# A layer that starts with four output tiles on unnormalised input, three narrow tiles, and waits that are moved

## What is computed

```python
def hybrid_layer(x, ...):
    proj = x @ w_in                       # 2048 -> 4928 columns
    (q_lat, kv_lat, k_rope, g_mla, p_in, g_pool, c_h, c_b, c_c, g_conv) = jnp.split(proj, ...)
    y_mla = mla_mixer(...) * silu(g_mla)  # latents are rms-normed, projected, 8 heads attend
    y_pool = pool_mixer(...) * silu(g_pool)
    y_conv = conv_mixer(...) * silu(g_conv)
    out = concat([y_mla, y_pool, y_conv]) @ w_out + b_out
    return layernorm(DEEPNORM_ALPHA * x + out, ln_g, ln_b)
```

## Time and profile before

| | us |
|---|---|
| median of three runs | 2517.47 |
| lowest, highest | 2517.44, 2517.75 |
| the profiled execution | 2517.92 |
| its span, first to last instruction | 2516.2 |
| PE busy in the span | 2426.2 (96%) |
| DVE, ACT, POOL busy | 1260.9, 890.5, 396.4 |
| mean granted clock of PE | 0.985 of full |

### The profile page before, as it was taken

The page is one execution under the profiler, slowest core; times in us unless marked ns, Lnnn a source line. Parts: engine busy times, 40 slices in busy tenths (PEclk is TensorE's granted clock), DMA queues, the critical chain, the costliest instruction groups (busy, mean ns, idle before and its releaser), DMA issues.

```text
span 2516.2 us, 31644 instructions
## 1 busy us (share of the span) xinstructions
PE 2426.2 (96%) x11582; PEld 1979.5 (79%) x11582; DVE 1260.9 (50%) x1789; ACT 890.5 (35%) x1344; POOL 396.4 (16%) x391
## 2 busy tenths in 40 slices
PE   4999999999999999999999998899999999999997
PEld 2778888788888778888788886688877888887886
DVE  8655544366446555544366546634245444444334
ACT  4422222365224422223365223422224444444221
POOL 6400000033003300000042003003001122122000
PEclk8999999999999999999999999999999999999999
DMA  3455554212222455553212222323221222222332
GB/s 140 154 168 176 174 178 132 83 59 67 92 92 67 156 175 170 181 181 127 80 55 69 92 90 101 126 92 100 92 92 59 84 75 81 76 76 97 129 100 75
DMA packets 78281, 277.70 MB, mean 110 GB/s; under 512 B 8832, under 2 KB 9088, under 8 KB 77824
## 3 DMA queue, kind: packets, MB, share of 16 engines
q1 hardware_dynamic: 61344, 213.29, 26.5%
q0 software_dynamic: 16864, 63.45, 7.5%
HBM read 268.31 MB, written 8.39 MB: 110 GB/s over the span
## 4 chain that ended last, share of the span: by engine, by line
PE 80%; issue 9%; DVE 6%; POOL 3%; ACT 2%; DMA 0%; DVEq 0%; ACTq 0%; SPq 0%; POOLq 0%
PE bank L309 25%; PE bank L311 25%; PE bank L310 25%; POOL sum L394 1%; DVE w_lo L304 1%; PE bank L1871 1%; DVE x_lo L1024 1%; POOL probs L381 1%; PE bank L1801 1%; ACT w_hi L294 1%; PE bank L1935 0%; DVE x_res L1577 0%; DVE squares L1030 0%; PE bank L1936 0%; PE bank L1786 0%
## 5 line engine op out<-in xcount | busy, mean ns | idle before, releaser
L311 PE MATMUL bank<-x_hi,w_hi 128*128 128x512 f32 x2928 | 1145.0, 391 | 0.0
L310 PE MATMUL bank<-x_hi,w_lo 128*128 128x512 f32 x2928 | 1143.4, 390 | 0.0
L309 PE MATMUL bank<-x_lo,w_hi 128*128 128x512 f32 (+1 forms) x2416 | 966.4, 400 | 33.2 <-DVE x_lo L1024 17.4
L304 DVE TENSOR_TENSOR w_lo<-w_raw,w_hi 128x1024 fp32r<-128x1024 f32 x390 | 491.7, 1263 | 827.0 <-ACT w_hi L294 825.9
L294 ACT ACTIVATE w_hi<-w_raw 128x1024 fp32r<-128x1024 f32 x390 | 407.5, 1048 | 964.9 <-PE bank L311 949.1
L311 PEld LDWEIGHTS bank<-x_hi,w_hi 128*128 128x128 f32 x2928 | 548.4, 187 | 120.6
L310 PEld LDWEIGHTS bank<-x_hi,w_lo 128*128 128x128 f32 x2928 | 549.7, 188 | 113.1 <-issue 2.4
L309 PEld LDWEIGHTS bank<-x_lo,w_hi 128*128 128x128 f32 (+1 forms) x2416 | 453.9, 188 | 132.4 <-issue 33.8
L309 PE MATMUL bank<-mix_lo,w_hi 128*128 128x512 f32 x640 | 252.8, 395 | 1.3 <-issue 1.0
L381 POOL TENSOR_SCALAR probs<-probs,stats 128x128 f32<-128x128 f32 (+3 forms) x128 | 138.7, 1090 | 679.1 <-DVE stats L1312 679.0
L309 PEld LDWEIGHTS bank<-mix_lo,w_hi 128*128 128x128 f32 x640 | 120.7, 189 | 27.2 <-issue 1.6
(11 more groups left out here) (296 smaller groups left out, 2207.5 us busy)
## 6 DMA issues: line engine op xcount, KB each, us to landing
w_raw<-stream SPq DMA_DIRECT2D x390, 512.0 KB, 3.5
ada_w<-wada POOLq DMA_DIRECT2D x96, 512.0 KB, 4.6
x_res<-xT SPq DMA_DIRECT2D x16, 256.0 KB, 5.4
x_res_spill<-x_res POOLq DMA_DIRECT2D x8, 512.0 KB, 7.5
x_res<-x_res_spill POOLq DMA_DIRECT2D x8, 512.0 KB, 7.2
outT<-x_res SPq DMA_DIRECT2D x16, 256.0 KB, 2.3
cond_b<-cond POOLq DMA_DIRECT2D x2, 1024.0 KB, 5.4
row_params<-rows POOLq DMA_DIRECT2D x1, 1536.0 KB, 7.4
```

Of the source, the lines that this page charges most:

```text
L304: nc.vector.tensor_tensor(out=WL[:, slot, :cols[n]], in0=RAW[:, slot, :cols[n]], in1=WH[:, slot, :cols[n]].bitcast(F32), op=ALU.subtract). ...
L309: nc.tensor.matmul(out, wh, xl, start=first, stop=False)
L310: nc.tensor.matmul(out, wl, xh, start=False, stop=False)
L311: return nc.tensor.matmul(out, wh, xh, start=False, stop=last)
```

## The change

**Four raw tiles.** Layer 1 no longer waits for the norm. With g and b the gain and offset of the norm, m the mean and r the inverse deviation of a token, W^T (g (y - m) r + b) = r (W^T (g y) - m W^T g) + W^T b. So tiles 0 to 3 run on g y, split in two parts by ACT (`raw_hi`, during the output tiles) and DVE (`raw_lo`), and DVE (`raw_tile`) and ACT apply m, r and the two weight sums to the results. W^T g and W^T b are made on PE from the unrounded weights, eight units of eight matmuls with two moving columns (`weight_sums`): four in the last two output tiles of layer 0, four in the raw tiles, where the totals and the spreads stand too. Tile 4 is the first on normalised input. Layer 1 swaps the two activation buffers (in its rows `x_lo` holds the rounded part and `x_hi` the rest), and four units of weights instead of three stand at its start.

**The norm's own work.** `x_res` is centred by POOL (14 tiles, `ysub`) ahead of the residual's add, in both layers, so that `centred` and the last correction of the shift leave DVE. In layer 1 a feature tile may be written only when the four raw tiles have used it (`raw_freed`).

**Narrow tiles.** The weights of a narrow tile are packed twice; DVE turns the second copy into the low part in place. One matmul with 128 (or 64) columns then makes hi and lo together, two matmuls per k instead of three, and DVE adds the two row groups afterwards. This concerns `T_KR` in both layers and `T2_F`.

**Waits moved.** The latent sums stand at k = 5 instead of 7 and their spread at 10 instead of 12 (in layer 1 one tile later), those of the second group at 15 instead of 7 and, in the next tile, 6 instead of 2. The spatial products stand at k = 7 to 14 of their tile instead of 0, 2, ..., 14. `q_lo` of the first pair comes before the gates. Slots are counted through, so that a unit waits for the third one before it everywhere.

```diff
+OUT_ORDER = (MIX_ORDER, list(range(16)))
...
+RAW_LAYER, RAW_TILES = 1, 4
+RAW_BANKS = (0, 3, 4, 6)
...
+        HI, LO = (XH, XL, XH), (XL, XH, XL)
+        OFF_HI, OFF_LO = (OFF_XH, OFF_XL), (OFF_XL, OFF_XH)
...
+        def raw_freed(k):
+
+            n = RAW_LAYER * LAYER_UNITS
+            if k % 8 == 7:
+                return w_used, n + RAW_TILES * (k // 8 + 1)
+            return S["raw_used"], k + 1 - k // 8
...
+                wide = narrow(l, s)
+                if wide:
+                    raw, both = (t[:, slot, :].rearrange("p (k c) -> p k c", c=P)[:, :, wide:2 * wide]
+                                 for t in (RAW, WH))
+                    nc.vector.tensor_tensor(out=both, in0=raw, in1=both.bitcast(F32), op=ALU.subtract)\
+                        .then_inc(w_lo, 1)
+                    continue
...
+                pool.wait_ge(S["sh_b"], l + 2)
+                for k in range(2, KT):
+                    nc.gpsimd.tensor_tensor(out=Y[:, k, :], in0=Y[:, k, :], in1=SB[:, :], op=ALU.subtract)\
+                        .then_inc(S["ysub"], 1)
...
+            def raw_hi(n, k):
+                nc.scalar.activation(HI[n][:, k, :], Y[:, k, :], ACT.Copy, scale=norm_cols(n, k)[0])\
+                    .then_inc(S["raw_hi"], 1)
...
+                    act.wait_ge(S["bc_m"], n)
+                    nc.scalar.activation(SB[:, :], PS[2][:, :], ACT.Copy).then_inc(S["sh_tot"], 1)
...
+                    if n == RAW_LAYER and k in (5, 6, 7, 8):
+                        split(n, 2 + (k - 5) // 2, ((k - 5) % 2,))
+                    elif n < DEPTH and n != RAW_LAYER and k in (11, 12):
                         split(n, 2, (k - 11,))
                     buf = NBUF[k % 4]
                     gain, offset = norm_cols(n, k)
                     act.wait_ge(S["n_mul"], KT * n + k + 1)
+                    if n == RAW_LAYER:
+                        act.wait_ge(*raw_freed(k))
...
+                raw = RAW_TILES if l == RAW_LAYER else 0
+                for i in range(raw):
+                    if i == 2:
+                        split(l, 5)
+                        act.wait_ge(S["cond_in"], 16 * (l + 1))
+                        nc.scalar.activation(CONDB[:, :], CONDB[:, :], ACT.Silu).then_inc(S["cond_silu"], 1)
+                        lat_sd(l, 0)
+                        act.wait_ge(S["lat_bc"], 2 * l + 1)
+                    act.wait_ge(S["lat_raw"], 2 * (i + 1))
+                    if i:
+                        act.wait_ge(S["sq_sum"], 4 * l + (0, 0, 1, 1)[i])
+                    nc.scalar.activation((T0, Y1)[i % 2][:, :], LAT[:, i, :], ACT.Square, scale=-1.0,
+                                         bias=VEC[:, 2 * i + 1:2 * i + 2]).then_inc(S["in_ev"], 1)
+                    nc.scalar.activation(LAT[:, i, :], LAT[:, i, :], ACT.Identity, scale=-1.0,
+                                         bias=VEC[:, 2 * i + 1:2 * i + 2]).then_inc(S["lat_hi"], 1)
+                    if i < 2:
+                        split(l, 4, (i,))
...
-                dve.wait_ge(S["bc_m"], n)
-                TT(out=SB[:, :], in0=SB[:, :], in1=PS[2][:, :], op=ALU.add).then_inc(S["sh_tot"], 1)
                 dve.wait_ge(S["bc_r"], n)
+
+            def raw_lo(n, k):
+                dve.wait_ge(S["raw_hi"], k + 1)
+                dve.wait_ge(w_used, n * LAYER_UNITS - (k < 8))
+                STT(out=LO[n][:, k, :], in0=Y[:, k, :], scalar=col(n - 1, C_LG + k), in1=HI[n][:, k, :].bitcast(F32),
+                    op0=ALU.mult, op1=ALU.subtract).then_inc(S["raw_lo"], 1)
+
+            def raw_sums():
+                dve.wait_ge(S["vec_mm"], 2 * RAW_TILES)
+                V.tensor_copy(VEC[:, :], PS[5][:, 2 * RAW_TILES:4 * RAW_TILES]).then_inc(S["vec_set"], 1)
+                dve.wait_ge(S["vec_set"], 1)
+                TT(out=VEC[:, :], in0=PS[5][:, 0:2 * RAW_TILES], in1=VEC[:, :], op=ALU.add).then_inc(S["vec_set"], 1)
+                dve.wait_ge(S["vec_set"], 2)
+
+            def raw_tile(l, t):
+                dve.wait_ge(w_used, first_done(l, t))
+                dve.wait_ge(S["n_x"], norm_uses(l, KT - 1))
+                STT(out=LAT[:, t, :], in0=SB[:, :], scalar=VEC[:, 2 * t:2 * t + 1], in1=PS[RAW_BANKS[t]][:, :],
+                    op0=ALU.mult, op1=ALU.subtract).then_inc(S["lat_raw"], 1)
+                dve.wait_ge(S["lat_raw"], 2 * t + 1)
+                TT(out=LAT[:, t, :], in0=LAT[:, t, :], in1=PS[7][:, :], op=ALU.mult).then_inc(S["lat_raw"], 1)
...
+                if raw:
+                    raw_sums()
+                    raw_tile(l, 0)
+                    split(l, 4, (0,))
+                    raw_tile(l, 1)
+                    split(l, 4, (1,))
+                    raw_tile(l, 2)
+                    raw_tile(l, 3)
+                    split(l, 5)
...
+                V.tensor_copy(LAT[0:ROPE, 6, :], PS[7][ROPE:P, :]).then_inc(S["kr_sum"], 1)
+                dve.wait_ge(S["kr_sum"], 2 * l + 1)
+                TT(out=PS[7][0:ROPE, :], in0=PS[7][0:ROPE, :], in1=LAT[0:ROPE, 6, :], op=ALU.add)                    .then_inc(S["kr_sum"], 1)
...
+                    if m == KT - 1 and l + 1 == RAW_LAYER:
+                        for k in range(8):
+                            raw_lo(l + 1, k)
...
+                        stat(l + 1, m)
+                    if m < KT - 1 or l + 1 == RAW_LAYER:
+                        split(l, T_OUT + m + 2, (1,))
+
+                for m in range(KT):
+                    out_tile(m)
+                if l + 1 == RAW_LAYER:
+                    for k in range(8, 12):
+                        raw_lo(l + 1, k)
+                    norm_end(l + 1)
+                    for k in range(12, KT):
+                        raw_lo(l + 1, k)
+                    normalise(l + 1, {k: (lambda k=k: split(l + 1, 2 + (k - 6) // 2, ((k - 6) % 2,)))
+                                      for k in range(6, 10)})
+                else:
+                    norm_end(l + 1)
+                    normalise(l + 1, {4: lambda: split(l, T_OUT + KT + 1, (1,))})
...
+                    q_lo(p)
...
+                    wide = narrow(l, s)
+                    if wide:
+                        both = WH[:, slot, col0:col0 + 2 * wide]
+                        nc.tensor.matmul(PS[bank][:2 * wide, :], both, xl, start=n == 0, stop=False)
+                        last = nc.tensor.matmul(PS[bank][:2 * wide, :], both, xh, start=False, stop=n == KT - 1)
+                    else:
+                        last = products(PS[bank][:, :], WH[:, slot, col0:col0 + P], WL[:, slot, col0:col0 + P],
+                                        xh, xl, n == 0, n == KT - 1)
...
+            def weight_sums(u):
+
+                slot, before, uses = unit(RAW_LAYER, u)
+                pe.wait_ge(raw_in[slot], 16 * uses)
+                c = (RAW_LAYER - 1) * LAYER_COLS + C_LG + 8 * (u // RAW_TILES)
+                for j in range(8):
+                    last = mm(PS[5][:, 2 * u:2 * u + 2], RAW[:, slot, j * P:(j + 1) * P],
+                              COL[:, c + j:c + j + C_LB - C_LG + 1:C_LB - C_LG], start=j == 0, stop=j == 7)
+                last.then_inc(S["vec_mm"], 1)
+
+            def raw_tiles(l):
+
+                tiles = range(RAW_TILES)
+                order = [(k, t) for k in range(2) for t in tiles[:-1]] + [(k, tiles[-1]) for k in range(2)]
+                order += [(k, t) for k in range(2, 6) for t in tiles]
+                order += [(k, t) for t in tiles for k in (6, 7)] + [(k, t) for t in tiles for k in range(8, 11)]
+                order += [(k, t) for k in range(11, KT) for t in tiles]
+                for k, t in order:
+                    half, col0 = k // 8, (k % 8) * P
+                    slot, before, _ = unit(l, RAW_TILES * half + t)
+                    if k % 8 == 0:
+                        pe.wait_ge(w_lo, before + 1)
+                    pe.wait_ge(S["raw_lo"], k + 1)
+                    if k == 0 and t == 0:
+                        pe.wait_ge(S["out_ev"], KT * l - 1)
+                    last = products(PS[RAW_BANKS[t]][:, :], WH[:, slot, col0:col0 + P], WL[:, slot, col0:col0 + P],
+                                    HI[l][:, k, :], LO[l][:, k, :], k == 0, k == KT - 1)
+                    if k % 8 == 7:
+                        last.then_inc(w_used, 1)
+                    elif t == RAW_TILES - 1:
+                        last.then_inc(S["raw_used"], 1)
+                    if t == RAW_TILES - 1:
+                        if k == 1:
+                            column_totals(l)
+                        elif k == 3:
+                            spreads(l)
+                        if 2 <= k < 6:
+                            weight_sums(RAW_TILES + k - 2)
...
-                    if m not in (T_KR, 3):
+                    raw = RAW_TILES if l == RAW_LAYER else 0
+                    if raw and m == T_KR:
+                        pe.wait_ge(S["lat_raw"], 2 * raw)
+                    elif raw and m == raw + 1:
+                        pe.wait_ge(S["in_ev"], taken(l, 0))
```

(32 more changed lines are left out.)

228 lines of the change are left out of this document (115 added, 113 removed).

## The result

The changed kernel is slower by 4.7 us: 2522.35 us median (2517.83 to 2524.89, 20 runs) against 2517.69 (2514.72 to 2519.85, 20 runs), ratio 1.0018, 95% interval 1.0011 to 1.0025. Forecast were 2528 and +10.6 us. The profiled execution took 2520.18 us, its span is 2518.5 with a mean clock of 0.985, so it is 2.3 us above the one of before.

A forecast was written before the change was run, and what follows sets the result against it. TensorE, busy 96% of the span, was taken as the bound: matmuls at 0.226 us plus waits and small work. Terms +20.4 - 3.7 + 2.4 - 1.5 - 7.0 = +10.6 us on 2517.9 gave 2528 us, range 2515 to 2535.

The forecast's parts named there:

- (c): PE's waits among layer 1's raw tiles, for split weights: 0.3 us plus 5, the latter between 1 and 7.
- the pair: First pair of the second block, reordered and with its narrow tile: -7.0 us, between -5 and -8.5.
- The start that was meant to be won is spent: Layer 1's start: 16.3 us without products went, 19 us of small matmuls came, the wait moved behind the raw tiles.
- (d): Layer 1's fifth tile, from PE's last raw product to the tile's end: 35.6 us, between 29 and 40.
- held until the fifteenth scaling: Case for the fifth tile's `w_lo` beside POOL's scalings: done 16.1 us after PE's last raw product, latent sums at 27.0.
- for five scalings again: Case for the fifth tile's `w_lo`: held over five scalings, done at 11.7 us, latent sums at 24.1.
- The wait that I called decisive: PE's wait for `w_lo` at layer 1's fifth tile: 8 to 16 us; under 5 would prove the forecast wrong.
- one operation's delay each: Second rival: fifth tile starts at 8.9 us, sums about 21, raw-tile waits 3; 2521.5 us, chance 0.25 with two other rivals.
- the first rival: No DVE-POOL collisions in layer 1: fifth tile starts at 8.2, sum at 19.2; 2518 us, chance 0.25 with two other rivals.
- low clock in (d): One stretch of low PE clock in layer 1's fifth tile, behind the latent sums: costs 1.5 us.
- The boundary of layer 1 and the second block: Centring leaves DVE, PE's 0.44 us wait goes, first subtraction starts 0.1 earlier: -1.5 us, between -0.5 and -2.5.
- Layer 0's low clock: Low PE clock behind the 2.65 us wait at layer 0's latent sums: 0 to 1.6 us, taken as 1.0.

The follow-up runs named there:

- the plain start: Changed kernel with the early start of layer 1 undone (three tiles behind its normalisation, as in layer 0), all else kept: 2500.71 us, ratio 0.9942 to the kernel before.
- the late scalings: Changed kernel with GpSimd's sixteen residual scalings held, in both layers, until the first latent sum of squares is added: 2514.91 us, ratio 0.9992 to the kernel before.
- the shifted ones: Four kernels with the plain start, GpSimd's scalings shifted by moved DMA load issues or added memsets: 2495.51, 2496.52, 2495.96 and 2493.98 us, one execution each.

## Why the prediction was right in its sign and wrong in its size

**What held.** PE has no gap ahead of the first raw tile. A unit of eight small matmuls is 1.70 us to the next product and 1.85 with the late restart behind it (predicted 1.8), the four in layer 0's last tiles 7.4 (7.3), the raw tiles 59.2 (59.7), the tiles behind them within 0.2. For the raw tiles this is partly luck: their waits are 3.2 us (0.55, 1.61, 0.49, 0.51) instead of the 5.3 of (c), and 1.7 us more went elsewhere. Narrow tiles give 3.8 us (3.7). The wait at the latent sums of layer 0 is 2.68 us (2.65), at the third spatial product 4.39 (4.5), and the third tile of the pair does not wait. "The start that was meant to be won is spent" stands: with the plain start the kernel is some 20 us faster.

**The step that failed: (d), the fifth tile.** The prediction had the new `w_lo` at 6.9 us behind PE's last raw product and "held until the fifteenth scaling" (16.1) or "for five scalings again" (11.7), and the latent sums at 27.0 or 24.1, taken as 25.6. Measured: weights there at 8.06 us, just at its own no-collision value of 8.2, and sums ready at 19.6. Six microseconds of the sum were a hold that did not come; with no collision at all, in the kernel with the late scalings, the sums are ready at 18.3. I took the two holds of the kernel before (4.70 us in layer 1, 4.83 in layer 0), both in the same arrangement, for a law of the scalings, though the row next to one of them (2.11 us, one operation) spoke the other way. The wait that I called decisive, "8 to 16 us", came out at 8.06: that test was badly set, since a start without any collision lies at its edge.

**Weighed against the rule.** What the traces show is a `w_lo` that meets a scaling and takes 1.24 to 1.79 us, with the following scaling stretched to 1.64 us or more; in the arrangement of before it takes 4.70 to 4.86, and 4.46 in one of the shifted ones. (The longest scaling of the earlier trace rows, 1.644 us, is stretched in the same way, by a `w_lo` that had been held.) The rule of the Trainium skill (page "SBUF — State Buffer", section "SBUF: two separate sides"), that the one which comes second is kept out "for the whole instruction", agrees with the first kind (1.54 us where it met a scaling with 0.46 us to go and takes 1.23 alone) and not with the second. The rival made from it, one operation's delay each, gave 2521.5 us with the start at 8.9, the sums at 21 and 3 us of waits in the raw tiles; measured are 8.06, 19.6, 3.2 and 2522.35. It had a chance of 0.25 together with two others; it should have been the forecast. That its sum is so near is partly luck: the start and the sums came almost where the first rival, no collisions, has them (8.2 and 19.2), and the low clock and the boundary, below, missed in opposite directions.

**A term that was too small: low clock in (d).** 1.5 us were set for one stretch. There are two, 852.5 to 863.0 (clock 0.51) and 869.5 to 877.0 (0.54). The first costs nothing of its own, since the second wait is behind it: with the first scalings of layer 0 shifted, PE's clock is full earlier in this tile, its wait is 5.80 instead of 4.74 us, and the sums are ready at the same 19.6. The second leaves 11.8 us where 10.0 were predicted, 1.8 more. So (d) is 31.5 us: 6.0 less by the collision, 1.8 more by the clock.

**The boundary of layer 1 and the second block: -1.5, measured -2.8.** The second subtraction is no longer stretched (1.26 us; 2.25 at the same place before), as predicted. But the first starts 1.85 us sooner behind PE's last product, not 0.1 (PE, then GpSimd, in the changed kernel):

```profile
1550.13 2.62 PE L1699 MATMUL bank<-ident 128*128 128x128 f32 x22
1552.59 1.84 PE L1708 MATMUL bank<-ones,sum 128*128 128x1 f32 x16
1554.29 1.58 PE L1699 MATMUL bank<-ident 128*128 128x128 f32 x12
1556.06 2.15 PE L1716 MATMUL bank<-diag,ones 128*128 128x128 f32 x16 [0.19 <-DVE diag L1076]
```

```profile
1557.94 1.26 POOL L408 TENSOR_TENSOR centred<-x_res,shift 128x512 f32<-128x512 f32 x1 [6.21 <-ACT shift L544]
1559.17 1.26 POOL L408 TENSOR_TENSOR squares<-x_res,shift 128x512 f32<-128x512 f32 x1
```

In the earlier trace rows, the same pattern one layer earlier, twelve fillers took 2.28 us and the spreads 2.92, and so they do at this place in the kernel before; here 1.58 and 2.15. Behind the 0.44 us wait for the sum the clock had been low. Without the wait it is full, in this kernel and at all 23 such boundaries of the experiments (fillers 1.58 or 1.59 us), and that is 1.4 us which the term left out.

**Layer 0's low clock: +1.0.** Nothing in this profile, 1.7 to 3.5 us in four of seven. As a mean some 1.7 us; the term was sound, a single profile cannot show it.

**Together.** Of the 5.9 us between +10.6 and +4.7, (d) is 4.1, the boundary 1.3, the raw tiles and the tiles behind them 0.5, and the pair takes 0.4 back; the 0.4 left is less than the interval of the ratio.

## What to carry to other kernels

A stall that is moved behind new work is often two stalls in a row, and mending the first alone feeds the second (8.06 and 4.74 us became 1.17 and 10.39): move the work of both. Before normalisation is pushed behind the products, price the small matmuls that carry its corrections at PE's full rate where PE has no slack (here four units, 7.4 us; four more lay where VectorE set the pace, and leaving them out gave nothing), and compare with what a plain start with well-placed side work already hides. A duration seen in one arrangement of two engines is a sample and no law: move one of them a little in time before building a forecast on it, as here a later start of GpSimd's scalings gave 7 us for one line of code.

## What the runs showed of the chip that I had not expected

- The same `w_lo` beside the same GpSimd operations takes 1.24 to 1.79 us or 4.46 to 4.86. Held ones end only with the last scaling or the one before. Neither VectorE's idle time (7.55 us in both kinds), nor the distance into the scaling, nor the number of scalings run decides it by itself.
- TensorE's clock behind a wait is not settled by the wait: after 2.6 us at the same place it stayed full in three profiled kernels and fell to half for 3.4 to 6.9 us in four; after 1.77 us it fell in one. The executions of the changed kernel (2517.8 to 2524.9 us) differ in their mean clock too, 0.986 in the shortest and 0.983 in the longest, and two profiles alone can mislead by 2 us.
- A wait of 0.44 us ahead of small matmuls had the low clock behind it at both layer ends of the kernel before (twelve fillers 2.28 us); without the wait, 1.58.
